# A hybrid SSD / S5 / mixture-of-experts layer: another order around the last chunk of the SSD scan

## The reference, cut to what matters

```python
proj = rmsnorm(x) @ w_in                       # z, xbc, dt, u
xbc = silu(causal_conv(xbc))                   # x, B, C of the SSD heads
y = ssd_chunked(x, dt, A, B, C, D, h0, 128)    # 16 heads, state 128, chunks of 128 tokens
y_ssd = rmsnorm(y * silu(z))
y5 = gelu(s5(u))                               # 64 groups, complex diagonal state
y_s5 = rmsnorm(y5 * sigmoid(y5 @ w_glu + b_glu))
x = x + concat(y_ssd, y_s5) @ w_out
x = x + hier_moe(rmsnorm(x))                   # 32 experts, two for each token
```

## Time and profile before

| | |
|---|---|
| time, median of 3 runs | 1090.63 us (1088.73 to 1094.45) |
| time of the profiled execution | 1094.45 us |
| its span, first to last instruction | 1092.6 us |
| mean granted clock of PE | 0.974 |
| PE busy | 984.4 us (90%) |
| DVE, ACT, POOL busy | 451.3, 310.5, 332.2 us |
| DMA | 277.54 MB, mean 254 GB/s |

### The profile page before, as it was taken

How to read it: one execution, slowest core, us unless ns; L and a number is a source line. 1 busy time by engine, 2 the same in 40 slices (tenths; PEclk the granted TensorE clock), 3 DMA queues, 4 the chain that set the end, 5 groups by cost and what they waited for, 6 DMA issues and landing times.

```text
span 1092.6 us, 17000 instructions
## 1 busy us (share of the span) xinstructions
PE 984.4 (90%) x6438; PEld 694.2 (64%) x6439; DVE 451.3 (41%) x674; ACT 310.5 (28%) x597; POOL 332.2 (30%) x534
## 2 busy tenths in 40 slices
PE   6999999999999996999999999999877778988881
PEld 5889789786776785998865555555444435544440
DVE  6999875444455999863251111111101011111103
ACT  3026223543323343232242223222221121221123
POOL 1000888888213994000012222222221111221110
PEclk9999999999999898999999999999999899999996
DMA  6584271120098533447299999999999999999954
GB/s 260 125 143 79 40 145 40 39 61 21 12 267 219 195 116 121 159 160 290 106 334 397 392 384 402 390 391 402 401 397 399 389 417 413 407 415 415 424 230 163
DMA packets 73564, 277.54 MB, mean 254 GB/s; under 512 B 36952, under 2 KB 38872, under 8 KB 56496
## 3 DMA queue, kind: packets, MB, share of 16 engines
q1 hardware_dynamic: 63020, 252.67, 62.9%
q0 software_dynamic: 8720, 19.86, 6.7%
q10 hardware_dynamic: 1780, 4.41, 1.1%
HBM read 260.17 MB, written 25.61 MB: 262 GB/s over the span
## 4 chain that ended last, share of the span: by engine, by line
PE 67%; DMA 21%; DVE 8%; issue 1%; ACT 1%; SPq 0%; ACTq 0%; POOLq 0%; POOL 0%; DVEq 0%
PE ps L658 21%; DMA sb_arena<-w_up 20%; PE ps L1026 8%; PE ps L1040 7%; PE ps L1019 7%; PE ps L923 7%; PE ps L993 2%; PE ps L777 2%; PE ps L690 1%; PE ps L803 1%; PE ps L746 1%; PE ps L828 1%; DVE sb_y_lo L1730 1%; PE ps L824 1%; DVE sb_arena L1749 1%
## 5 line engine op out<-in xcount | busy, mean ns | idle before, releaser
L658 PE MATMUL ps<-sb_arena 128*128 128x264 f32 (+1 forms) x1152 | 272.7, 398 | 11.3 <-DMA sb_arena<-wi 8.7
L658 PEld LDWEIGHTS ps<-sb_arena 128*128 128x128 f32 x1152 | 222.4, 195 | 61.6 <-issue 9.6
L1917 DVE TENSOR_TENSOR sb_s5b<-sb_s5b,ps 128x256 f32<-128x256 f32 x36 | 22.4, 623 | 416.5 <-PE ps L1026 416.5
L1026 PE MATMUL ps<-sb_arena 128*64 128x256 f32 x1152 | 137.5, 393 | 27.7 <-DMA sb_arena<-w_up 27.7
L1040 PE MATMUL ps<-sb_arena 128*64 128x512 f32 x576 | 131.5, 598 | 19.2 <-DVE sb_arena L1921 19.2
L1019 PE MATMUL ps<-sb_arena 128*64 128x256 f32 x1152 | 131.2, 380 | 15.6 <-DMA sb_arena<-w_gate 12.2
L1026 PEld LDWEIGHTS ps<-sb_arena 128*64 128x64 f32 x1152 | 85.1, 142 | 76.4 <-DMA sb_arena<-w_up 34.5
L1019 PEld LDWEIGHTS ps<-sb_arena 128*64 128x64 f32 x1152 | 83.1, 137 | 74.7 <-DMA sb_arena<-w_gate 23.1
L1370 ACT ACTIVATE sb_kxf<-ps,sb_gate_of 64x512 f32<-64x512 f32 x36 | 24.6, 682 | 311.7 <-PE ps L1040 311.7
L614 POOL COPY sb_idc<-sb_tok_of 64x1 int32 x36 | 6.4, 177 | 292.2 <-DMA sum_scr<-sb_kxf,sb_rwc 274.9
L1040 PEld LDWEIGHTS ps<-sb_arena 128*64 128x64 f32 x576 | 38.7, 136 | 88.9 <-issue 61.2
(11 more groups left out here) (308 smaller groups left out, 1269.4 us busy)
## 6 DMA issues: line engine op xcount, KB each, us to landing
sb_arena<-w_gate SPq DMA_DIRECT2D x32, 2048.0 KB, 34.2
sb_arena<-w_up SPq DMA_DIRECT2D x32, 2048.0 KB, 40.4
sb_arena<-w_down SPq DMA_DIRECT2D x32, 2048.0 KB, 32.8
sb_arena<-wi SPq DMA_DIRECT2D x28, 512.0 KB, 3.9
sb_arena<-w_out SPq DMA_DIRECT2D x4, 2048.0 KB, 7.9
sb_arena<-ssm_in POOLq DMA_DIRECT2D x8, 512.0 KB, 8.9
sb_arena<-wglu SPq DMA_DIRECT2D x8, 512.0 KB, 6.7
o_ssm_s<-sb_arena POOLq DMA_DIRECT2D x8, 512.0 KB, 4.2
```

The source lines that it names most:

```text
L658: last = mm(ps[:, b0 + h, 0:t1 - t0], ring[w % 3][:, k, :], src[:, k, t0:t1], start=k == 0, stop=k == KD - 1)
L1026: last = mm(ps[64 * r:64 * r + 64, 1, 0:256], xt[:, k, :], Wu[s][:, k, 256 * r:256 * r + 256], start=k == 0, stop=k == KD - 1)
L1917: V.tensor_tensor(hh.rearrange("p (j c) -> p c j", j=2), sg.rearrange("p (c j) -> p c j", j=2), ps[:, 1, 0:256].rearrange("p (c j) -> p c ...
```

## The change

POOL issues none of the loads of the states 0 to 3 before the second half of the S5 outputs has been written (`y5_st[1]`), and then all four together; all eight states are now waited for as a group of four (`h0s_ld` at 64). PE runs wide block 27 ahead of `ssd_c(3)` and block 28 directly behind it, ahead of chunk 4, with one wait more (`yo_ev` at 6) and one fewer (`wide_free[1]` at 14). ACT runs the GELU before `b_tokens(4)` and `segment_exp(4)`, with one small exponential between. DVE runs `sample_c` for 0 to 2 ahead of the outputs of chunk 3, 3 to 5 behind its state, 6 and 7 ahead of the outputs of chunk 4, where before it ran 0 and 1 behind the state of chunk 3, 2 to 5 ahead of the outputs of chunk 4, and 6 and 7 behind its state.

```diff
@@ POOL
             pl.dma_start(bcf, bc_scr.rearrange("b c -> (b c)").partition_broadcast(P)).then_inc(bc_ld, 16)
-            for b in range(2):
+            pl.wait_ge(y5_st[1], 16 * 9)
+            for b in range(4):
                 pl.dma_start(h0b[b], hin[b]).then_inc(h0s_ld[0], 16)
             pl.wait_ge(bc_ld, 16)
-            pl.wait_ge(h0s_ld[0], 32)
-            pl.wait_ge(y5_st[1], 16 * 9)
-            for b in range(2, 4):
-                pl.dma_start(h0b[b], hin[b]).then_inc(h0s_ld[0], 16)
@@ PE
             wide(26)
+            pe.wait_ge(yo_ev, 6)
+            wide(27)
             ssd_c(3)
-            wide(27)
+            wide(28)
             ssd_a(4)
-            pe.wait_ge(wide_free[1], 14)
             ssd_b(4)
             ssd_y_off(4)
-            wide(28)
             pe.wait_ge(yo_ev, 8)
             wide(29)
             ssd_c(4)
@@ ACT
-            b_tokens(4)
-            segment_exp(4)
             for i in range(8):
                 if i % 4 == 0:
                     ac.wait_ge(yraw_ld[i // 4], 16)
                 act_(yg[:, i, 0:NP_].rearrange("p (m j) -> p j m", j=J),
                      yraw[:, i, 0:NP_].rearrange("p (j m) -> p j m", j=J), ACT.Gelu_apprx_tanh)
                 act_(yg[:, i, NP_:N], yraw[:, i, NP_:N], ACT.Gelu_apprx_tanh).then_inc(gelu_done, 1)
+            link(act_(gate_of[:, 0:1], ones[:, 0:1], ACT.Exp))
+            b_tokens(4)
+            segment_exp(4)
@@ DVE, sample_c
-                dv.wait_ge(h0s_ld[b // 4], 32 if b < 2 else 64)
+                dv.wait_ge(h0s_ld[b // 4], 64)
@@ DVE, the loop over chunks, ahead of the wait for y_mm
-                for b in ((2, 3, 4, 5) if c == 4 else ()):
+                for b in ((0, 1, 2) if c == 3 else (6, 7) if c == 4 else ()):
                     sample_c(b)
@@ DVE, behind the state
                 if c == 3:
-                    for b in range(2):
-                        sample_c(b)
-                if c == 4:
-                    for b in range(6, NS):
+                    for b in range(3, 6):
                         sample_c(b)
```

## The result

The changed kernel takes 1102.15 us (median of 4 runs, 1101.26 to 1105.17), the kernel before took 1091.25 beside it (4 runs): a ratio of 1.0103, with a 95% interval of 1.007 to 1.0137. That is 10.9 us more, where 1103 was forecast. The profiled execution took 1108.28 us, span 1106.4, 13.8 more than the profiled one of before; it is longer than the four timed ones, as that of before was the longest of its runs.

A forecast was written before the change was run, and what follows sets the result against it. PE bounds the kernel up to the expert loop, then DMA, shifted in full. Out projection +13.4, less 1 for its clock: +12.4, so 1094.45 becomes 1106.9; the median, 3.8 lower, 1103; 8 in 10: 1094 to 1110.

The forecast's parts named there:

- the saving of 1 us: Start of the out projection: 1 us of idling instead of 7.8 should save some 1 us of half clock.
- POOL's loads: Loads of states 0 to 3: `y5_st[1]` at 341.7, 3 us earlier; the fourth load issued by 345.2.
- The landing: Arrival of the four states: last one 10.3 us after issue, all down at 355.5, bounds 350 and 359.
- the sum: Whole kernel: out projection 13.4 us later, less 1 for its clock, +12.4 in all; 1106.9 in the profiled execution.
- The one price of 5.3: Second read-back of the S5 outputs: 5.3 us to land, at 347.0, so GELU paces block 28 a little.
- the first wait: PE between block 28 (end 351.8) and chunk 4: idle 16 us until DVE's state of chunk 3 at 367.7.
- The second wait: PE ahead of block 29: idle from 372.2 to 378.1, while DVE runs samples 3 to 5 and `off_diagonal`.
- the cold case: Rival: chunk 4 and block 29 wholly at half clock, `ssd_c(4)` ends 398 to 401, +16 to +19; chance 0.20.
- Where both meet: Ahead of the out projection: DVE ready about 438.5, PE decides, start at 441.4 instead of 428.0, +13.4.
- The relief: DVE's tail: products and `low_parts` get lighter by some 4 us, as POOL's loop ends sooner against DVE's work.
- The samples beside POOL: Rival: six samples beside POOL's loop each lose half a scaling of 2.91 us more, sum some 9 us longer; chance 0.05.
- the later loop of POOL: POOL's loop ends at 431.8 instead of 422.4, 5 us sooner against DVE's work than now.

The follow-up runs named there:

- e1: Kernel before with only POOL's part of the change: states 0 to 3 loaded together after the S5 stores, every sample waiting for all four; 1102.76 us, 1.0125.
- e2: Changed kernel with loads, sample waits and DVE's list as before; only the orders on PE and ACT are new; 1093.63 us, 1.0045.
- e3: Changed kernel with the four state loads issued early, at 316 us, without the wait for the stores; 1092.49 us, 1.0029.
- e6: Changed kernel plus 36 unused matmuls between block 28 and chunk 4, filling PE's first idle stretch; 1104.58 us, 1.014.
- e7: Changed kernel, loads still late, samples reordered to 4, 5, 6, then 7, 0, 1, then 2, 3; POOL in the old order; 1098.21 us, 1.0069.
- e9: Kernel before with one more wait: POOL's loop over the states starts only behind the third sample; 1098.89 us, 1.0075.
- e4: Kernel before with samples 4 and 5 moved into DVE's hole and none left behind the state of chunk 4; 1087.17 us, 0.9983.

## Why the prediction was right

**The mechanism.** It went by the steps that were written down, shown by e1 to e3: the late loads alone carry most of the loss (the load of `w_gate` 11.7 us late, of 13.3), the order of PE and ACT adds little (2.6 alone), and early loads take all of it back at that place and most of it in the median. The out projection was forecast to start 13.4 us later and did so by 14.8; the saving of 1 us from its start at full clock came out as 1.3 (the expert loop starts 13.5 later, 578.23 against 564.73) to 1.4 (from out to the load 109.3 us against 110.7).

**POOL's loads.** `y5_st[1]` let the loads go at 339.7, forecast 341.7: two loads less ahead of the stores freed 5 us and not 3. The landing took the gain back: the two ring loads, the read-back and the four states are under way together (DMA share 1.03 in 345 to 350 us), the median state landed 12.0 us after its issue, and the second read-back took 9.5 us where I had taken the 5.3 of the earlier trace rows. The last state was down at 357.00, 13.5 us after the queue had issued it (339.97 + 3.54), where the sum had 10.3; forecast 355.5, bounds 350 to 359. That the two errors, 1.7 us too late and 3.2 too short, nearly cancel is luck. The one price of 5.3 came from a read-back that had only two ring loads and two states beside it.

**DVE and the first wait.** State of chunk 3 done at 368.15, forecast 367.7. Samples 0 to 2 took 2.63 each, less than the 2.96 assumed; POOL's loop begins only at 359.63, beside the second of them. PE: block 28 ended at 354.6, forecast 351.8, as the GELU waited for that second read-back (PE idles 2.17 us for it); the wait was thus 13.77 and not 16, at no cost, since its end is set by DVE.

**The second wait.** It ended at 379.04, forecast 378.1. The length was 3.24 us instead of 6: chunk 4 ran at half clock and ended at 375.8, not 372.2. Windows of the changed kernel (us; busy PE, PEld, DVE, ACT, POOL; granted clock; DMA share; GB/s):

```profile
366.00:372.00 6.00, 3.53 (x22) 1.98 (x22) 5.93 (x10) 0.75 (x4) 5.73 (x4) 0.50 0.29 87
372.00:378.00 6.00, 3.71 (x6) 0.43 (x4) 5.83 (x6) 5.95 (x5) 5.68 (x3) 0.50 0.17 53
378.00:380.00 2.00, 0.96 (x2) 0.84 (x3) 1.97 (x4) 1.62 (x3) 1.92 (x2) 0.50 0.35 104
384.00:388.00 4.00, 4.00 (x19) 3.39 (x18) 4.00 (x4) 0.00 (x0) 3.60 (x4) 1.00 0.44 131
```

The granted clock is 0.50, the level of 1.2 GHz, through chunk 4 and at the start of block 29 (379.04), and 1.00 in the last row. `ssd_c(4)` ended at 395.96, forecast 394.8; the cold case would have been 398 to 401. The 3.4 us of work at half clock that the sum allows for block 29 rest on no row of the trace of before; block 29 took 9.65 us, 2.3 more than the 7.39 of block 26 at full clock. The rule of the Trainium skill (TensorE: Matmul & The Clock Gate, HAM oscillation) says that an array that falls back to half clock in the waits between bursts of matmuls starts each burst cold. The rows agree for chunk 4. Between chunk 4 and block 29 the clock had not risen, so here the two waits make one cold stretch and not two restarts; in e6, where it is at 1.00 in chunk 4, it is at 0.50 again behind the wait of 6.14 us. What a restart costs is another matter, and e6 shows it for the first one: nothing, as the engine that sets the pace is DVE. The second lies on PE's own chain, which goes on to the out projection without a wait, so its 2.3 us count.

**Where both meet.** DVE's tail started at 397.27, forecast 396.0. PE came last, as forecast, and DVE's `low_parts` were done at 439.7, a microsecond later than the 438.5 forecast. The relief was put at "some 4 us" and was 3.8 (9.01 and 5.58 against 10.72 and 7.66). So far the sum holds. The mis-sized terms cancel but for 1.4 us; the largest is the landing.

**The samples beside POOL** did not get dearer than the mean of before: 2.63 and 3.1 (377.46 less 368.15, for three) against 2.96.

**What the prediction did not see.** It treated the later loop of POOL as a gain, since its end moves less than DVE's tail. That is right for this change, and right only because DVE is late by more. e7 and e9 show the other side. Beside a DVE that is in time, a POOL loop that starts 13.1 us later costs 7.0 us by itself (e9); in e7 it starts 10.8 us later, and the kernel loses 8.6. A repair of the changed kernel that looks at DVE's list alone (e7) wins 2.3 us of 10.9 by the medians, 4.8 of 13.3 by the place of the load.

**The median.** The medians differ by 10.9 and the profiled executions by 13.8. The profiled execution of the changed kernel is 3.1 us above the highest of its four timed ones; its mean granted clock is 0.962, theirs 0.966 to 0.973. Both profiled executions have the half-clock stretch of the last section. Whether the timed ones have it is not known, as they left no trace. The forecast took 3.8 us off the profiled sum, from the times of before alone; in the changed kernel the difference is 6.1 (1108.28 less 1102.15). So the nearness of 1103 to 1102.15 is in part luck: the sum for the profiled execution was 1.4 us too low (1106.9) and what was taken off it 2.3 too little. What the profiled execution of the changed kernel lost against the timed ones, and where, stays open.

## What to carry to other kernels

Before a load is moved behind a wait, look at what stands behind its consumer in the in-order list of the waiting engine: here outputs whose matmuls were through by 344.5 waited 20 us for data that they don't use, and PE waited for them. Fill a hole with work whose inputs have landed, and let the engine that follows (POOL) take the same order. Where two engines slow each other, the time at which the second one runs is a cost of its own, to be summed like a wait.

## What the runs showed of the hardware

**DVE and POOL share something that sets the cost of DVE's products.** `low_parts`, eight instructions with two inputs in SBUF, took 5.58 us wherever POOL's loop was over (seven profiles; 5.59 in one of them), and 7.66, 9.32, 13.89 and 15.54 us as more of them fell beside it; the four products took 2.58 alone and 11.57 beside it. One profile shows both: in e9 the five instructions of `low_parts` that lie beside the loop take up 2.34 to 3.18 us each, from start to start, and those behind it 0.69. That is 1.7 to 2.5 us more for each, about one POOL instruction (1.92 to 2.69 us there). The Trainium skill (SBUF — State Buffer, Who interferes with whom) says that a DVE instruction with two SBUF inputs and a POOL instruction that reads SBUF block each other for a whole instruction; by these numbers the trace agrees. POOL pays too: beside DVE's gate and its `wo_lo`, instructions of 6.75 and 6.13 us from 386.19 on in e9, two of POOL's took 5.00 and 5.97 us instead of 1.92 and 1.91.

**A half-clock stretch that only some executions have.** Ahead of the edit, near 190 us, behind matmuls of 16 columns, the granted clock is 0.50 in the profiles of before and of the changed kernel and 1.00 in e4, whose code is the same up to there. The windows of before, and of e4:

```profile
189.00:193.00 4.00, 4.00 (x13) 3.16 (x13) 1.05 (x5) 0.00 (x0) 3.21 (x11) 0.50 0.00 0
```

```profile
189.00:193.00 4.00, 4.00 (x18) 3.36 (x19) 1.31 (x5) 0.00 (x0) 3.22 (x11) 1.00 0.00 0
```

Block 26 starts at 321.9 to 322.1 in the four profiles that have it in full, at 319.1 in one that has half of it (e6), and at 317.6 to 318.7 in the eight without. It is the largest single part that I found of the up to 4.5 us by which block 26 moves between profiles. The timed executions of one kernel differ by 1.5 to 7 us; that the stretch is a part of this too is likely and not shown, as they left no trace. It is a reason to compare places from a common start and not by the span.
